# First weight unit asked for behind one tile of x, its remainder split in halves and its remainder products last in each tile

## What is computed

```python
def mixer_streams(x, pos, w_in, b_gate):
    z = jnp.einsum('btd,de->bte', x, w_in).astype(jnp.float32)
    mq, mk, mv, mo, mi, mf, aq, ak, av, iq, ik, iw = jnp.split(z, split_points, axis=-1)
    ...
    q = partial_rope(heads(aq, A_HEADS), pos)
    k = partial_rope(heads(ak, A_HEADS), pos)
    v = heads(av, A_HEADS)
    qi = partial_rope(heads(iq, IDX_HEADS), pos) * (IDX_DIM ** -0.5)
    ki = partial_rope(ik[:, :, None, :], pos)[:, :, 0, :]
```

## Time and profile before

| | us |
|---|---|
| median of 3 runs | 1720.71 |
| lowest and highest run | 1719.81, 1722.46 |
| the profiled execution | 1719.58 |
| its span | 1717.4 |
| PE busy | 1613.3 (94%) |
| DVE busy | 778.1 (45%) |
| ACT busy | 467.3 (27%) |
| POOL busy | 412.6 (24%) |

### The profile page before, as it was taken

One profiled execution on the slowest core, in us unless ns is written; L12 is line 12 of the kernel. 1 busy time (PEld: TensorE's weight loads), 2 busy tenths in 40 slices (PEclk: granted clock), 3 DMA queues, 4 the chain that ended last, 5 costly groups with the idle time before them and its releaser, 6 DMA issues.

```text
span 1717.4 us, 27522 instructions
## 1 busy us (share of the span) xinstructions
PE 1613.3 (94%) x10804; PEld 1483.5 (86%) x10804; DVE 778.1 (45%) x1682; ACT 467.3 (27%) x948; POOL 412.6 (24%) x388
## 2 busy tenths in 40 slices
PE   6989999999999995979999999999999999999983
PEld 6955999999996664558779999999999999999983
DVE  2046899999205662255365223133232331322337
ACT  3365222211225562126144211111112112121013
POOL 3530444212210000105277221122221122222004
PEclk9979999999999998899999999999999999999997
DMA  5200212232317105113311211111111111110002
GB/s 173 57 26 0 86 41 66 63 98 94 99 47 240 26 26 173 50 37 118 126 50 47 69 33 50 51 50 50 50 29 46 51 50 50 50 45 30 25 1 101
DMA packets 116781, 110.38 MB, mean 64 GB/s; under 512 B 15906, under 2 KB 101542, under 8 KB 116658
## 3 DMA queue, kind: packets, MB, share of 16 engines
q1 hardware_dynamic: 116658, 108.61, 20.4%
HBM read 88.61 MB, written 19.95 MB: 63 GB/s over the span
## 4 chain that ended last, share of the span: by engine, by line
PE 51%; DVE 2%; issue 1%; ACT 0%; DVEq 0%
PE bank L1614 30%; PE bank L1592 15%; PE bank L1395 6%; DVE y_tm L1826 1%; DVE stats L1801 1%; PE bank L1535 0%; DVE y_tm L1829 0%; PE bank L1758 0%; DVE y_acc L1600 0%; ACT y_tm L1776 0%; PE bank L992 0%; PE bank L1023 0%; DVE moments L1807 0%; DVE hidden L1685 0%; ACT silu L1655 0%
## 5 line engine op out<-in xcount | busy, mean ns | idle before, releaser
L1614 PE MATMUL bank<-x_split,gate_up_split 128*128 128x352 f32 x3168 | 510.9, 323 | 3.5 <-DVE hidden L1685 2.5
L1614 PEld LDWEIGHTS bank<-x_split,gate_up_split 128*128 128x128 f32 x3168 | 507.4, 188 | 4.4 <-DVE hidden L1685 3.1
L2067 PE MATMUL bank<-w_split,xT_split 128*128 128x256 f32 (+1 forms) x2160 | 268.9, 283 | 7.3 <-POOL w_split L2273 7.3
L1592 PE MATMUL bank<-hidden_split,weight_split 128*128 128x352 f32 x1584 | 259.3, 324 | 9.8 <-DVE y_acc L1600 7.7
L2067 PEld LDWEIGHTS bank<-w_split,xT_split 128*128 128x128 f32 (+1 forms) x2160 | 257.0, 180 | 10.5 <-issue 8.2
L1592 PEld LDWEIGHTS bank<-hidden_split,weight_split 128*128 128x128 f32 x1584 | 256.1, 189 | 11.0 <-DVE y_acc L1600 8.6
L1685 DVE TENSOR_TENSOR hidden<-silu,bank 128x352 f32<-128x352 f32 x66 | 34.4, 521 | 413.2 <-ACT silu L1655 413.1
L1720 POOL TENSOR_TENSOR gate_up_split<-gate_up,gate_up_split 128x2048 fp32r<-128x2048 f32 x22 | 104.3, 4740 | 377.4 <-ACT gate_up_split L1647 377.4
L1600 DVE TENSOR_TENSOR y_acc<-y_acc,bank 128x352 f32<-128x352 f32 x264 | 137.3, 521 | 110.4 <-PE bank L1592 109.1
L2362 DVE TENSOR_SCALAR_CACHE_REDUCE chosen<-scores,level 128x384 uint8<-128x384 f32 (+2 forms) x198 | 174.3, 943 | 1.2
L2126 PE MATMUL bank<-xT_split,w_split 128*128 128x352 f32 x864 | 138.5, 323 | 0.0
(11 more groups left out here) (254 smaller groups left out, 1643.1 us busy)
## 6 DMA issues: line engine op xcount, KB each, us to landing
w_unit<-in_w_in_dram SPq DMA_DIRECT2D x16, 1024.0 KB, 5.6
gate_up<-in_w_gate_dram SPq DMA_DIRECT2D x22, 512.0 KB, 4.0
gate_up<-in_w_up_dram SPq DMA_DIRECT2D x22, 512.0 KB, 5.3
down_weight<-in_w_down_dram SPq DMA_DIRECT2D x11, 1024.0 KB, 5.4
scratch_dram<-feature_stage SPq DMA_DIRECT2D x36, 176.0 KB, 1.8
scores<-in_x_prompt_dram SPq DMA_DIRECT2D x8, 512.0 KB, 5.2
out_dram<-stage SPq DMA_DIRECT2D x32, 128.0 KB, 1.7
out_weight<-in_w_out_dram SPq DMA_DIRECT2D x16, 256.0 KB, 6.4
```

What stands on the lines that cost most here:

```text
L1592: mm = pe.matmul(PS[6 + n % 2][:, 0:CH], wds[:, a, k, d * P:(d + 1) * P], hs[:, 2 * s + k, b, c * CH:(c + 1) * CH], start=(k == 0 and (a, ...
L1614: mm = pe.matmul(PS[2 * c + w][:, 0:CH], gs[u][:, a, w, k, :], xs[:, b, k, c * CH:(c + 1) * CH], start=(k == 0 and (a, b) == PARTS[0]), st ...
L2067: mm = pe.matmul(bank[0:rows(i), 0:HALF], xs1[:, a, k, tile_cols(i)], w[:, b, k, :], start=(k == 0 and (a, b) == PARTS[0]), stop=(k == KD ...
```

## The change

It edits only the head of the first stage.

- SP asks for weight unit 0 behind the first tile of x, where it stood behind three.
- ScalarE splits unit 0 behind two evictions of x, where it stood behind six.
- The remainder of unit 0 is halved over its eight row blocks k: VectorE writes blocks 0 to 3 between its work on tile 0 and tile 1 (a new semaphore, `w_lo_first`), GpSimd blocks 4 to 7.
- In the product jobs of unit 0 the sixteen products with the high part of w come first and the eight with its remainder last. The job waits for the high part, and waits for the two halves of the remainder only in front of the products that read them.
- In the job list the products of unit 0 start behind tile 1 (`i >= 1`), where they started behind tile 2.

```diff
         for i in range(TILES):
             jobs += [("xT", i, 0), ("xT", i, 1)]
-            if i >= 2:
+            if i >= 1:
                 jobs += first_unit[:2]
                 first_unit = first_unit[2:]
...
                 if n:
                     sp.wait_ge(w_lo, n)
+                if n == 1:
+                    sp.wait_ge(w_lo_first, 1)
...
-            for i in range(3):
+            load_x(0)
+            load_w(0)
+            for i in range(1, 4):
                 load_x(i)
-            load_w(0)
-            load_x(3)
...
-                        pe.wait_ge(w_lo, unit_no[g, u] + 1)
                         w = wsplit[unit_no[g, u] % 2]
+                        terms = [(k, a, b) for k in range(KD) for a, b in PARTS]
+                        if unit_no[g, u] == 0:
+                            terms.sort(key=lambda term: term[2])
+                            pe.wait_ge(w_hi, 1)
+                        else:
+                            pe.wait_ge(w_lo, unit_no[g, u] + 1)
 
                         pe.wait_ge(x_low, 2 * i + 2)
-                        for k in range(KD):
-                            for a, b in PARTS:
-                                mm = pe.matmul(...)
+                        for k, a, b in terms:
+                            if unit_no[g, u] == 0 and (k, b) == (0, 1):
+                                pe.wait_ge(w_lo_first, 1)
+                            if unit_no[g, u] == 0 and (k, b) == (4, 1):
+                                pe.wait_ge(w_lo, 1)
+                            mm = pe.matmul(...)
...
-            high_before = {6: [0], pos["tm", "iq", 0, 6]: [1]}
+            high_before = {2: [0], pos["tm", "iq", 0, 6]: [1]}
...
                 pool.wait_ge(w_hi, n + 1)
-                hi, lo = wsplit[n % 2][:, 0], wsplit[n % 2][:, 1]
-                pool.tensor_tensor(lo, wraw[n >= 4], hi.bitcast(F32), ALU.subtract).then_inc(w_lo, 1)
+                k = slice(0 if n else 4, KD)
+                hi, lo = wsplit[n % 2][:, 0, k], wsplit[n % 2][:, 1, k]
+                pool.tensor_tensor(lo, wraw[n >= 4][:, k], hi.bitcast(F32), ALU.subtract).then_inc(w_lo, 1)
...
             for n in range(2 * TILES):
                 i, j = divmod(n, 2)
+                if n == 2:
+                    dve.wait_ge(w_hi, 1)
+                    dve.tensor_tensor(wsplit[0][:, 1, 0:4], wraw[0][:, 0:4], wsplit[0][:, 0, 0:4].bitcast(F32), ALU.subtract)\
+                        .then_inc(w_lo_first, 1)
```

More of the change, by code:

```diff
@@ L183, in build @@
         w_in_s, w_hi, w_lo = sem("w_in"), sem("w_hi"), sem("w_lo")
+        w_lo_first = sem("w_lo_first")
         wsm_in, wsm_hi, wsm_lo = sem("wsm_in"), sem("wsm_hi"), sem("wsm_lo")
@@ L2060, in _ @@
                     else:
-                        pe.wait_ge(w_lo, unit_no[g, u] + 1)
                         w = wsplit[unit_no[g, u] % 2]
-                        pe.wait_ge(x_low, 2 * i + 2)
-                        for k in range(KD):
-                            for a, b in PARTS:
-                                mm = pe.matmul(bank[0:rows(i), 0:HALF], xs1[:, a, k, tile_cols(i)], w[:, b, k, :],
-                                               start=(k == 0 and (a, b) == PARTS[0]),
-                                               stop=(k == KD - 1 and (a, b) == PARTS[-1]))
+                        terms = [(k, a, b) for k in range(KD) for a, b in PARTS]
[4 more added lines that the diff above has]
+                            pe.wait_ge(w_lo, unit_no[g, u] + 1)
+                        pe.wait_ge(x_low, 2 * i + 2)
+                        for k, a, b in terms:
[3 more added lines that the diff above has]
+                                pe.wait_ge(w_lo, 1)
+                            mm = pe.matmul(bank[0:rows(i), 0:HALF], xs1[:, a, k, tile_cols(i)], w[:, b, k, :],
+                                           start=((k, a, b) == terms[0]), stop=((k, a, b) == terms[-1]))
                 elif kind == "ikf":
```

## The result

| | before | changed |
|---|---|---|
| median of 20 runs | 1720.49 us | 1723.62 us |
| lowest and highest | 1718.09, 1722.46 | 1720.87, 1726.23 |
| the profiled execution | 1719.58 us | 1723.20 us |
| its span | 1717.4 us | 1721.1 us |
| mean granted clock | 0.974 | 0.975 |

The ratio is 1.002 with a 95% interval of 1.0013 to 1.0027, so 2.2 to 4.6 us. The sign was as forecast, and the new waits came where they were forecast. The size was 3.1 us where 7.0 was forecast. The prediction had given 0.11 to a change of under 0.2% and 0.83 to a larger loss.

A forecast was written before the change was run, and what follows sets the result against it. TensorE, busy 94% of the span, was taken to bound the kernel. New tile waits of 12.4 us less a head gain of 5.4 made it 7.0 us slower, 1727.7 us from 1720.71; range 1722 to 1735.

The forecast's parts named there:

- What the moved jobs add: Tiles 2 to 8: TensorE waits for each tile's eviction and split, 1.9 us six times plus 1.0, 12.4 us in all.
- Gain of the head: Kernel start: first product moves from 18.59 to 12.4 us; less 0.79 us for tile 2's transposes, gain 5.4 us.
- I take the low clock of the first products as before: First products: the low clock was assumed to stay, since TensorE idles before tile 1 too; no gain counted.
- So nothing is given back there: TensorE sets that point, before and after: At 95.32 us, behind the small-weight jobs: unit 3's lateness hides none of TensorE's delay; nothing taken off.
- rival 4: Tiles and head: waits 1.5 us a tile, head gains 6.4, unit 1's path hides the rest; 1721 to 1724, chance 0.09.
- One sign that the prediction had named for itself: End of the kernel: the forecast is wrong if the difference at 100 us is not there at the end.
- The head wins: Head and tiles: 5.4 us gain stays and tile waits are small, 0.2 us each; 1716.7 us, chance 0.06.
- The clock falls in the gaps: Tile pattern: TensorE's clock drops in the new gaps, adding 6 to 19 us; 1734 to 1747, chance 0.13.
- The row that was set against it: At 788 to 797 us: TensorE busy 5.90 of 9.0 us, one 2.6 us gap, granted clock stayed at 1.00.
- The weights come no sooner: Head: transfers in flight share the engines, so the gain is 4.0 and the loss 8.4 us; 1729.1, chance 0.08.
- New waits at no cost: Unit 0's first products: sixteen high products, at least 2.05 us, cover the waits on both remainder halves; cost nothing.

The follow-up runs named there:

- experiment 1: Changed kernel with only the job list put back, so unit 0's products start behind tile 2 again; 1714.84 us, ratio 0.9967.
- experiment 2: Kernel before with only the job list changed, and ScalarE's split of unit 0 behind four evictions; 1729.73 us, ratio 1.0062.
- experiment 7: The second execution: the changed kernel run once more, unedited, to look at the clock; one execution, 1726.15 us.
- experiment 10: Changed kernel with weight unit 3 asked for after six of sixteen index pages; 1724.9 us, ratio 1.0025.
- experiment 12: Changed kernel with VectorE's half of unit 0's remainder behind tile 1's two x remainders; one execution, 1720.73 us.
- experiment 6: Kernel before with GpSimd's remainder of weight unit 2 moved behind two more rotary steps; 1720.79 us, ratio 1.0008.
- experiment 9: Kernel before with GpSimd's unit 2 remainder behind two more rotary steps and unit 3 asked for after six of sixteen index pages; 1717.8 us, ratio 0.999.
- experiment 3: Changed kernel with unit 0's products in the old order, both remainder halves waited for before the first; 1726.16 us, ratio 1.0041.
- experiment 4: Changed kernel with a job list that starts early but puts every tile's products behind the next tile's transposes; 1713.6 us, ratio 0.996.
- experiment 5: Changed kernel with unit 0's whole remainder written by GpSimd, none by VectorE; 1724.77 us, ratio 1.0028.
- experiment 8: Experiment 4's kernel with GpSimd's remainder of unit 2 moved behind two more rotary steps; 1715.46 us, ratio 0.9973.

## Why the prediction was right in its mechanism and wrong in its size

**"What the moved jobs add", 12.4 us: right.** The period was forecast at 5.8 us and is 5.84. The waits stand where they were put, and each of six tiles costs 1.91 us. The way to 1.9 holds an error: 1.77 + 0.26 is 2.03. The step from VectorE to TensorE took 0.15 us (31.09 + 1.29 = 32.38 to 32.53), less than the 0.26 taken over from GpSimd, so the rounding down was luck. The loss between 26 and 59 us was 13.4. Without the clock's 1.5 (tile 7) that is 11.9, and the 0.5 missing to 12.4 is a TensorE wait on GpSimd's rotary step that the kernel before has in the same stretch and the changed one has not: behind the 32-row job that starts at 49.12 the transposes start after 3.34 us (52.46), behind the one at 78.46 after 2.90, and the next product is late by 0.1 more. Experiments 1 and 2 show that this term belongs to the job list and to nothing else.

**"Gain of the head", 5.4 us: too small by 1.3.** The changed profile gives 6.7. The first product came at 11.80 rather than 12.4. And "I take the low clock of the first products as before" was wrong: 48 products took 6.50 us, where before they took 7.21. The second execution (12.59 and 6.93) gives a gain of 5.5. The mean of the two is 6.1 (6.0 with the profiles of experiments 10 and 12, which start in the same way), so this step was off by some 0.7 us on average.

**"So nothing is given back there: TensorE sets that point, before and after": the step that failed.** It read one profile, in which unit 3's path and TensorE's own had ended together at 95.32, and took the tie for a bound by TensorE alone. The term for what a later TensorE hides was put at nothing, and it was 1.8 us in the profiles. Two things were missed. First, TensorE's waits on GpSimd's rotary steps cost the kernel before 0.5 us near 52 and 1.1 us at 63.01 (of which 0.90 is the wait that the row shows). They were not priced at all, and they went when TensorE came 7 us later. Second, unit 3, behind SP's index pages, holds the kernel before (by 0.19 us in its profile) and does not hold the changed one, whose ScalarE had 1.69 us to spare. The traces show both. The medians agree, less sharply: taking the wait at 63.01 away alone gave nothing (experiment 6), taking it and unit 3's lateness away gave 2.0 us (experiment 9, interval 0.2 to 3.3), and unit 3 early gave the changed kernel nothing (experiment 10). This was rival 4 in kind, though it named other places.

**The sum with measured terms.** At the first transposes behind the small-weight jobs (95.32 before): 12.4 less 6.7 (head), less 1.6 (the two waits on GpSimd), less 0.2 (unit 3), plus 1.5 (the clock in tile 7) is 5.4 us for the first profiled execution of the changed kernel, and 12.4 less 5.5, 1.6 and 0.2 is 5.1 for the second. The profiles show 5.5 and 5.0, so the terms close there. For an average execution it is an estimate: with 6.1 for the head the sum is 4.5, the clock adds 1.5 in two profiles of seven, 0.4, and unit 3 holds the kernel before by some 0.8 us more, as the page issue took 31.67 us in its profile and 32.5 in the mean of the eleven profiles that have all 32 pages in one loop (before, changed, experiments 1 to 8 and 12). That leaves 4.1 us against 3.1 measured, inside the interval of 2.2 to 4.6. The rest is not settled. The one profile of the kernel before may hold it: each of the eleven other kernels that have a median stands worse against it at this place than by the medians, by 0.4 to 3.3 us (the changed kernel 5.5 and 5.0 against 3.1, experiment 4 6.0 ahead against 6.9). One sign that the prediction had named for itself came true with this: the difference at 100 us, 5.5, was not all there at the end.

**The rivals.** "The head wins" is wrong as put, but experiment 4 shows where it would have been right: with no waits on the tiles, at 1713.6, near the 1714.0 that 1720.7 - 6.7 would say. "The clock falls in the gaps" is partly right: one tile, 1.5 us, in two of seven profiles. The row that was set against it, a clock that stayed high over one gap of 2.6 us, was no proof for seven gaps. The Trainium skill's rule on this (TensorE: Matmul & The Clock Gate, "A second HAM failure mode: psum-queue depth-cycling") tells of a clock that goes back and forth; here it fell once in two executions and not at all in five. "The weights come no sooner" is wrong: they came at 8.86.

**New waits at no cost.** That the products' new waits cost nothing holds: no row of the profile shows a TensorE wait on either half of the remainder. GpSimd's half took 3.42 us, though, not 2.25, and ended at 14.27, not 13.2; the products in front of those that need it covered that too. The order of the products earns it (experiment 3, 2.5 us); what the halving adds lies between nothing and some 2 us (experiment 5).

## What to carry to other kernels

When a job list is shifted so that work starts sooner, look at what stood between a producer and its consumer in the steady part. Here the transposes of the next tile and the products of the tile before covered each tile's eviction and split, and a shift of one tile took that cover away seven times, at 1.9 us a full tile. Delaying one product job at the start (experiment 4) kept both the early start and the cover. And when a forecast makes the main engine later, read the waits that it has now behind the edited part: those that it hides by coming later are given back. And where two paths end together in one profile, moving one of them may gain nothing.

## What was not expected of the hardware

- VectorE holds GpSimd up when both subtract with two SBUF inputs. GpSimd's 1024 a partition took 3.42 us (3.39 to 3.42 in eight profiles) beside VectorE's subtraction of 1.23 us, and 2.37 us without it (one profile), though VectorE's remainders of x, which read one input from PSUM, lay beside it then. The Trainium skill says this (SBUF — State Buffer, section "Who interferes with whom": a VectorE instruction with two SBUF inputs contends with a GpSimd instruction that reads SBUF), and the runs agree. VectorE's own half took its 1.22 to 1.23 us either way. So halving the remainder in parallel ended it 3.4 us after the split, not 2.3.
- TensorE's slow stretch at the first products differs between executions with the same head: 48 products took 6.50, 6.93, 7.18 and 7.08 us in four profiles (changed, experiments 7, 10 and 12). In each the first products start 0.21 us apart and the others 0.12; the slow ones were about 5, 10, 12 and 11. The kernel before has the same spacing of 0.21 us in its first 13 products, in a window whose granted clock is 0.57 (18.5 to 22.0). The granted clock of 11.8 to 18.0 reads 1.00 in all four, so the column does not show this stretch.
